# Turning the first key tiles later: an order table of a three-layer transformer kernel on TensorE

## The reference

```
h  = modulate_2(rms_norm_2(x, p['norm1']), sh1, sc1)
hc = modulate_2(rms_norm_2(xc, p['norm1']), csh1, csc1)
q  = rms_norm_2(split_heads(h @ w_q), q_gain)
k  = rms_norm_2(split_heads(h @ w_k), k_gain)
v  = split_heads(h @ w_v)
kc = rms_norm_2(split_heads(hc @ w_k), k_gain)
vc = split_heads(hc @ w_v)
y  = neighbourhood_attention(q, k, v, kc, vc, rpb) @ w_o
```

## Time and profile before

| | before |
|---|---|
| time, median of 3 runs | 1103.03 us (1101.34 to 1104.34) |
| profiled execution | 1102.09 us |
| its span | 1100.3 us |
| mean granted TensorE clock | 0.992 |
| PE busy | 1070.0 us, 97% |
| DVE busy | 773.2 us, 70% |
| ACT busy | 547.2 us, 50% |
| POOL busy | 114.3 us, 10% |

### The profile page before, as it was taken

The page is one execution under the profiler, slowest core; times in us unless marked ns, Lnnn a source line. Parts: engine busy times, 40 slices in busy tenths (PEclk is TensorE's granted clock), DMA queues, the critical chain, the costliest instruction groups (busy, mean ns, idle before and its releaser), DMA issues.

```text
span 1100.3 us, 20336 instructions
## 1 busy us (share of the span) xinstructions
PE 1070.0 (97%) x8042; PEld 973.7 (88%) x8042; DVE 773.2 (70%) x1293; ACT 547.2 (50%) x932; POOL 114.3 (10%) x133
## 2 busy tenths in 40 slices
PE   6899999999999999999999999899999999999998
PEld 2889778999999989888999999788866889999998
DVE  2688776688787678846677775787449667666665
ACT  4642576444443574655444444536347555454442
POOL 1102004000000027510000000300331010000000
PEclk9999999999999989999999999999999999999999
DMA  9971374798888716465777775484530135645541
GB/s 370 413 295 58 117 250 133 272 364 314 349 328 324 264 58 238 165 267 200 273 274 269 264 287 191 137 310 162 140 86 31 40 116 173 205 158 191 175 168 39
DMA packets 68594, 232.91 MB, mean 212 GB/s; under 512 B 12144, under 2 KB 12432, under 8 KB 68144
## 3 DMA queue, kind: packets, MB, share of 16 engines
q1 hardware_dynamic: 62496, 227.27, 57.9%
q0 software_dynamic: 5888, 3.73, 1.6%
q10 hardware_dynamic: 144, 1.05, 0.3%
HBM read 230.91 MB, written 1.05 MB: 211 GB/s over the span
## 4 chain that ended last, share of the span: by engine, by line
PE 86%; DVE 6%; DMA 4%; issue 2%; ACT 1%; POOL 1%; SPq 0%; DVEq 0%; POOLq 0%; ACTq 0%
PE bank L1685 25%; PE bank L1687 24%; PE bank L1686 24%; PE bank L2186 3%; DMA a_raw<-ada 2%; DMA w_raw<-weights 2%; PE bank L1847 1%; PE bank L1741 1%; DVE bank L1194 1%; PE bank L1712 1%; PE bank L1870 1%; PE bank L1781 1%; PE bank L1856 1%; PE bank L1767 1%; PE bank L2061 1%
## 5 line engine op out<-in xcount | busy, mean ns | idle before, releaser
L1685 PE MATMUL bank<-h_hi,w_hi 128*128 128x256 f32 (+1 forms) x1424 | 411.7, 289 | 6.0 <-DVE h_lo L1163 3.1
L1687 PE MATMUL bank<-h_hi,w_lo 128*128 128x256 f32 (+1 forms) x1424 | 407.0, 286 | 0.0
L1686 PE MATMUL bank<-h_lo,w_hi 128*128 128x256 f32 (+1 forms) x1424 | 406.9, 286 | 0.0
L1080 DVE TENSOR_TENSOR w_lo<-w_raw,w_hi 128x1024 fp32r<-128x1024 f32 x271 | 329.5, 1235 | 82.3 <-ACT w_hi L660 81.0
L660 ACT CAST w_hi<-w_raw 128x1024 fp32r<-128x1024 f32 x271 | 277.5, 1045 | 97.9 <-PE bank L1687 86.2
L1685 PEld LDWEIGHTS bank<-h_hi,w_hi 128*128 128x128 f32 x1424 | 273.7, 192 | 15.3 <-issue 9.2
L1686 PEld LDWEIGHTS bank<-h_lo,w_hi 128*128 128x128 f32 x1424 | 273.8, 192 | 1.7 <-issue 0.5
L1687 PEld LDWEIGHTS bank<-h_hi,w_lo 128*128 128x128 f32 x1424 | 273.7, 192 | 1.3
L1685 PE MATMUL bank<-g_hi,w_hi 128*128 128x256 f32 x544 | 154.7, 284 | 0.1
L1686 PE MATMUL bank<-g_lo,w_hi 128*128 128x256 f32 x544 | 153.9, 283 | 0.0
L1687 PE MATMUL bank<-g_hi,w_lo 128*128 128x256 f32 x544 | 153.9, 283 | 0.0
(11 more groups left out here) (174 smaller groups left out, 1221.5 us busy)
## 6 DMA issues: line engine op xcount, KB each, us to landing
w_raw<-weights SPq DMA_DIRECT2D x281, 512.0 KB, 4.6
a_raw<-ada SPq DMA_DIRECT2D x140, 512.0 KB, 5.4
vals<-ada SPq DMA_DIRECT2D x4, 512.0 KB, 8.5
a_raw<-rpb POOLq DMA_DIRECT2D x9, 224.0 KB, 15.3
bias<-rpb POOLq DMA_DIRECT2D x7, 224.0 KB, 8.1
xT<-xt SPq DMA_DIRECT2D x1, 1024.0 KB, 8.5
big<-ctx SPq DMA_DIRECT2D x1, 1024.0 KB, 14.6
big<-ctx ACTq DMA_DIRECT2D x1, 1024.0 KB, 5.3
```

The source lines that it names most:

```text
L1080: nc.vector.tensor_tensor(w_lo[:, s, :], w_raw[:, s, :], w_hi[:, s, :].bitcast(fp), SUB)\
L1685: nc.tensor.matmul(out, a_hi, b_hi, start=start, stop=False)
L1686: nc.tensor.matmul(out, a_hi, b_lo, start=False, stop=False)
L1687: return nc.tensor.matmul(out, a_lo, b_hi, start=False, stop=stop)
```

## The change

The table `TURNED` has other steps for four of the twelve units. Tiles 0 and 1 stand at s=4 instead of s=1, tile 2 at s=5 instead of 4, tile 3 at s=6 instead of 5. With them go the head copies on ScalarE: those of tiles 0 and 1 from step 3 to 6, tile 2 from 6 to 7, tile 3 from 7 to 8. The tiles from 4 on are where they were, and so is everything else.

```diff
--- before.py
+++ after.py
@@ -92,7 +92,7 @@
 
 UNITS = 12
 SQUARED = {1: (0, 1), 4: (2, 3), 8: (4, 5), 10: (6, 7), 13: (8, 9), 16: (10, 11)}
-TURNED = {1: (0, 1), 4: (2,), 5: (3,), 9: (4,), 10: (5,), 12: (6,), 13: (7,), 15: (8, 9), 17: (10, 11)}
+TURNED = {4: (0, 1), 5: (2,), 6: (3,), 9: (4,), 10: (5,), 12: (6,), 13: (7,), 15: (8, 9), 17: (10, 11)}
 
 
 def ada_issue_table():
```

## The result

The changed kernel took **1095.54 us** (median of 5, 1093.81 to 1096.67) against 1102.79 us (median of 5, 1101.34 to 1104.34) of the kernel before. The ratio is 0.9937, with a 95% interval of 0.9924 to 0.995. The forecast was 1096.3, range 1094.0 to 1099.0.

What follows compares the result with a forecast made beforehand. TensorE (PE), busy 97% of the span, was taken to bound the kernel. Gain 7.64 less 0.88 is 6.76 us (4.67 wait, 2.09 clock); from the median 1103.03 that gives 1096.3, range 1094.0 to 1099.0.

Steps and rivals of the forecast that it cites:

- (a, b): At s=1, removing PE's stall and clock loss gives 7.64 us; tiles 0 and 1 cost 0.88 at s=4; net 6.76.
- The sentence that no row here shows this variation: On s=1's clock loss: the 2.09 us could differ in the next execution, by the skill's rule, though no row shows it.
- The estimate of 2.17: Clock penalty behind the s=1 stall by the skill's rule: 4.33 us x 0.5 = 2.17, against 2.09 from the trace.
- (c): Blocks s=2 to s=4 can start at once; low parts are ready 2.1 us ahead, the fifth split 6.4 ahead.
- (d): At tile 2, the narrowest place: scaled at 725.6, PE comes at 726.8, a cover of 1.2 us.
- (e): At tile 4, PE comes at 744.1; VectorE's scaling keeps a cover of 3.9 us, 4.4 before.
- (f): Banks 4 and 5 and ScalarE's order: head copies of tiles 0 and 1 at 726.6 to 728, cover 10 us.
- (g): From 716 us to the end: nothing known there is tied to a fixed time, so the shift should arrive whole.
- R1: Rival: the wait moves to tile 2, 1 to 3 us, time 1097.3 to 1099.3; chance 0.07.
- R2: Rival: slower, tile 2's wait drops the clock and eats the gain from 4.67 us on; 1104 to 1108; chance 0.03.
- R3: Rival: only the 4.67 us wait is gained, not the clock; time 1098.4; chance 0.05.
- R4: Rival: the gain is given back later, in the attention or at weight slots or bias tiles; 1101 to 1103; chance 0.05.

Runs made afterwards that it cites:

- e0: The changed kernel measured again, unaltered, beside other kernels: 1095.31 us, ratio 0.9943 to the kernel before.
- e3: The changed kernel with tiles 0 and 1 at s=3 instead of s=4: 1094.64 us, ratio 0.9935 to the kernel before.
- e9: The kernel before, unchanged, run once more for another trace: 1100.55 us, one run.
- e1: The changed kernel with tiles 2 and 3 put back at s=4 and s=5: 1101.06 us, ratio 0.999 to the kernel before.
- e6: The changed kernel with VectorE's two modulation sums of s=5 pulled to s=4, ahead of tile 2's row sums: 1096.05 us, ratio 0.9947 to before.
- e4: The changed kernel with tiles 0 to 3 all at s=7: 1099.72 us, ratio 0.9982 to the kernel before.
- e2: The changed kernel with tiles 0 and 1 at s=2 instead of s=4: 1097.88 us, ratio 0.9961 to the kernel before.
- e5: The kernel before, its tile order kept, with no modulation sums at s=0 and 1 and two at each of s=2 to 7: 1099.1 us, ratio 0.9976.
- e11: The kernel of e5 run again for another trace: 1099.72 us, one run.
- e10: The kernel of e2 run again for another trace: 1097.08 us, one run.

## Why the prediction was right

**The stall and its price (a, b).** 6.76 us was the sum, 6.75 the measured distance, and e0 and e3 repeat it. The reading of where the time lay, from the neighbours at full step, was sound. The split was less firm than it looked: 4.67 of wait and 2.09 of clock in the trace of before, 5.0 and 1.4 in another trace of the same kernel (6.41 together). The total lost was therefore itself 0.3 us different from execution to execution, and that the forecast met the distance to 0.01 us is luck. The sentence that no row here shows this variation is answered: e9 shows it. The estimate of 2.17 counted the 4.33 us in which PE works. The granted clock had fallen earlier, while PE still waited: it is 0.50 in the whole of 712.0 to 718.5, with PE busy in 4.25 of these 6.5 us.

**s=2 starts at once (c).** It does. PE has no gap from s=1 on.

**Tile 2 as the next late thing (d).** Foreseen cover 1.2 us, measured 1.4. e1 shows what the place costs when it is missed (the whole gain), e6 that the cover is 1.3.

**Tile 4 (e).** Foreseen cover 3.9, measured 4.2.

**Banks and head copies (f).** The copies of tiles 0 and 1 run from 727.61 to 728.86, that is 726.3 to 727.5 in the time of the trace of before; 726.6 to 728 was said. Nothing waits for them. e4 shows that the dependence is real once they stand at s=9.

**Nothing given back (g).** 319.35 and 319.36 us from the last tiles to the end. In e4, though, a second clock loss of 1.56 us appeared in the attention without any change there, so that stage is not free of chance.

**Median against profile.** The forecast went by the median of before. The measured 1095.54 is 0.8 under it, within the spread of either median.

**The rivals.** R1 and R2 didn't happen; e1 is R1 at full size, and it came to no gain, not to a loss. R3 is out, since 6.75 us is the wait and the clock's part together, and no fall came elsewhere in the stretch. R4 is answered under (g). The prices of the rivals were not all sound. R1 priced a wait of 1 to 3 us without the clock. In e2 the clock fell after waits of 1.6 and 0.3 us by the brackets, and 2.2 us of wait cost 3.85; in e5, e6 and e11 waits of this size cost nothing beside themselves. R2's break-even of 4.67 us goes with a clock part of 2.09. In e1 that part was 2.7, and a wait of 4.0 already took 6.64 of the 6.76.

## What to carry to other kernels

When an engine that bounds the kernel waits in an order written by hand, ask what stands ahead of the awaited instruction in the other engine's queue, and place the consumer behind that; then ask the same of the next consumers, because with PE earlier they are short in turn (e1 lost everything for want of one block). The admissible places form a window, here s=3 to somewhere short of 7, closed on the early side by the scaling (0.5 us of cover at s=3) and on the late side by the bank. For effects under 1% read the distance between two landmarks in the traces: here it came out at 45.91, 45.92 and 45.87 us where PE does not wait, and within 0.35 us where it does (52.66 and 52.32; 49.74 and 50.08), while the position of the first landmark shifts by five.

## What the runs showed of the hardware

**The clock.** PE's granted clock fell behind waits (by the brackets) of 4.5 us (before), 4.4 and 0.3 (e9), 3.8 (e1), 2.7 (e4), and 1.6 and 0.3 (e2 and e10, twice alike), and stayed up behind 1.8, 0.3 and 1.3 (e5), 2.1, 0.3 and 1.3 (e11), and 1.2 (e6). It also fell once behind waits of 0.8 and 0.7 us (e4, in the attention), where the same waits of the change had no fall. So the length of the wait alone does not decide between 1.6 and 2.1 us. A fall cost 1.4 to 2.7 us beside the wait. In the trace of before the clock was down when PE went on; in e9, e2 and e10 the first tile behind the wait still took 0.63 us, and the second was the slow one (0.94 to 1.09). The Trainium skill (TensorE: Matmul & The Clock Gate, Terms) has the penalty as the throttled time times (1 - K/N). The trace of before agrees if only the 4.33 us in which PE works count (2.17 by it, 2.09 by the rows); with the whole time at the lower level, 6.8 us by the granted clock, it would be 3.4.

**Plain float32 matmuls.** A matmul of constants with 512 columns is two records in the trace and takes 0.86 us in the stream (718.95 - 710.37 for ten), against 0.2265 us for one in the rounded format that the products use.
